# A two-block transformer in one kernel: the Fourier transforms' matrices loaded into X's place beside the projection

## What is computed

```python
def fourier_mix(u):
    B, S, _ = u.shape
    ug = u.reshape(B, S, F_GROUPS, F_GROUP_DIM).astype(jnp.float32)
    f = jnp.fft.fft2(ug, axes=(1, 3), norm="ortho").real
    return f.reshape(B, S, F_WIDTH).astype(u.dtype)

for l in range(DEPTH):
    last = l == DEPTH - 1
    h_x = modulate(x, sh1, sc1)
    h_c = modulate(xc, csh1, csc1)
    p_x = h_x @ lw["w_in"]
    p_c = h_c @ (lw["w_in"][:, :KV_COLS] if last else lw["w_in"])
    kv_c = kv_parts(p_c, lw, None)
    kv_x = kv_parts(p_x, lw, rope)
    ...
    mix_x = mixer(p_x, kv_all, lw, rope)   # y_f = fourier_mix(f_in) @ w_fo, and two attentions
    x = layer_norm(alpha * x + g1 * mix_x, ln1_g[l], ln1_b[l])
    ...
```

## Time and profile before

| | us |
|---|---|
| median of 3 runs | 3669.7 |
| lowest, highest | 3660.38, 3669.87 |
| profiled execution, time | 3670.66 |
| profiled execution, span | 3668.9 |

### The profile page before, as it was taken

The page is one execution under the profiler, slowest core; times in us unless marked ns, Lnnn a source line. Parts: engine busy times, 40 slices in busy tenths (PEclk is TensorE's granted clock), DMA queues, the critical chain, the costliest instruction groups (busy, mean ns, idle before and its releaser), DMA issues. The chain is left out here.

```text
span 3668.9 us, 37531 instructions
## 1 busy us (share of the span) xinstructions
PE 3231.2 (88%) x15004; PEld 2485.7 (68%) x15004; DVE 1937.6 (53%) x2904; ACT 1008.2 (27%) x1752; POOL 909.5 (25%) x596
## 2 busy tenths in 40 slices
PE   7988998999989999977898999599979778787698
PEld 4955666777478888775565664388869556576576
DVE  3654763444735555654474555467663546332354
ACT  3124761000221111221464001222231145411252
POOL 1003764221200000010377342200010326103353
PEclk9999999999999999989999999799989869788789
DMA  6411004443121111031102553222212200022100
GB/s 204 139 41 26 9 27 127 110 111 112 55 67 49 69 69 69 23 126 59 26 19 77 146 146 126 84 92 92 94 51 98 104 4 12 23 75 86 49 1 23
DMA packets 208413, 268.23 MB, mean 73 GB/s; under 512 B 29312, under 2 KB 136784, under 8 KB 207728
## 3 DMA queue, kind: packets, MB, share of 16 engines
q1 hardware_dynamic: 206160, 265.83, 22.7%
q10 hardware_dynamic: 2080, 0.01, 0.0%
HBM read 255.17 MB, written 10.52 MB: 72 GB/s over the span
## 5 line engine op out<-in xcount | busy, mean ns | idle before, releaser
L731 POOL TENSOR_TENSOR ht_lo<-HT,ht_hi 128x1024 fp32r<-128x1024 f32 x28 | 68.5, 2447 | 1144.5 <-ACT ht_hi L713 751.0
L1807 PE MATMUL ps<-ht_hi,w_hi 128*128 128x512 f32 (+1 forms) x768 | 275.4, 359 | 47.0 <-DVE w_lo L1925 32.9
L1807 PE MATMUL ps<-ht_lo,w_hi 128*128 128x512 f32 (+1 forms) x768 | 274.3, 357 | 0.0
L1807 PE MATMUL ps<-ht_hi,w_lo 128*128 128x512 f32 (+1 forms) x768 | 274.0, 357 | 0.0
L1817 PE MATMUL ps<-w_hi,a_hi 128*128 128x512 f32 x640 | 251.5, 393 | 4.3 <-DVE a_lo L1921 4.3
L1817 PE MATMUL ps<-w_lo,a_hi 128*128 128x512 f32 x640 | 250.5, 391 | 0.0
L1817 PE MATMUL ps<-w_hi,a_lo 128*128 128x512 f32 x640 | 250.3, 391 | 0.0
L363 PE MATMUL ps<-w_lo,ht_hi 128*128 128x320 f32 (+2 forms) x800 | 243.8, 305 | 0.0
L363 PE MATMUL ps<-gate_ht_hi,gate_w_hi 128*128 128x512 f32 (+1 forms) x576 | 228.4, 397 | 16.7 <-POOL w_lo L386 16.7
L1432 POOL TENSOR_TENSOR p_lo<-ring,p_hi 128x512 fp32r<-128x512 f32 x156 | 200.0, 1292 | 117.1 <-DVE p_hi L1387 88.6
L363 PE MATMUL ps<-U,ring 128*128 128x512 f32 (+1 forms) x576 | 217.9, 521 | 0.0
(11 more groups left out here) (394 smaller groups left out, 7964.1 us busy)
## 6 DMA issues: line engine op xcount, KB each, us to landing
ring<-w_dram SPq DMA_DIRECT2D x30, 2048.0 KB, 8.2
U<-w_ada_dram SPq DMA_DIRECT2D x80, 512.0 KB, 3.7
ring<-w_in_dram SPq DMA_DIRECT2D x48, 512.0 KB, 6.6
ring<-w_in_dram SPq DMA_DIRECT2D x8, 1280.0 KB, 5.9
ring<-a_w_in_dram SPq DMA_DIRECT2D x8, 1280.0 KB, 6.6
ring<-w_ada_dram SPq DMA_DIRECT2D x4, 2048.0 KB, 10.8
hi_scratch<-ht_hi SPq DMA_DIRECT2D x2, 3072.0 KB, 10.7
gate_ht_hi<-hi_scratch SPq DMA_DIRECT2D x8, 768.0 KB, 4.4
```

The lines of the kernel that those rows point to most:

```text
L731: pool.tensor_tensor(HT_LO[:, :, tokens], HT[:, :, tokens], HT_HI[:, :, tokens].bitcast(F32), ALU.subtract).then_inc(ht_ready.sem, 1)
L1807: last = pe.matmul(ps[:, g % 4, 0:c1 - c0], lhsT, rhs, start=(k + j == 0), stop=(k == KD - 1 and j == 2))
```

## The change

`DFT` becomes a view of `X` (its first four tiles). The two loads move from `fourier` into a new function, `fourier_loads`, called between the two projections; they wait for the normalised rows (`xn_ready`) and for the store of x, and raise a semaphore of their own, `dft_loaded`. The second projection loses its closing barrier. In its place TensorE waits for `dft_loaded` and for all evictions before the transforms, and VectorE waits for all evictions before the first half of its work.

```diff
--- before.py
+++ after.py
@@ -163,7 +163,7 @@
         MIX = view(0, KD, T)
         at_ot = NT * GATE_COL
         OT = view(at_ot, KD, T)
-        DFT = view(at_ot, 2 * XT, S)
+        DFT = X[:, 0:XT, :].rearrange("p t (a n) -> p (t a) n", n=S)
         at_ft = at_ot + KD * T
         FT = view(at_ft, 4, T)
         CTT = view(at_ft + 4 * T, 4, T)
@@ -203,6 +203,7 @@
         hi_ready = signal("hi_ready")
         ht_ready = signal("ht_ready")
         hi_stored = signal("hi_stored")
+        dft_loaded = signal("dft_loaded")
         hi_back = signal("hi_back")
         scales_ready = signal("scales_ready")
         wo_loaded = signal("wo_loaded")
@@ -812,6 +813,15 @@
         AB = view(at_ft + 4 * T, 2, S)
         TRIG = view(at_ft + 4 * T + 2 * S, 2, P)
 
+        def fourier_loads(now):
+
+            sp = nc.sync
+            sp.wait_ge(xn_ready.sem, now.xn + NT)
+            sp.wait_ge(x_stored.sem, x_stored.n)
+            sp.dma_start(DFT, A["dft_tokens"].rearrange("(t p) n -> p t n", p=P)).then_inc(dft_loaded.sem, 16)
+            sp.dma_start(TRIG[:, :, :], A["dft_features"].rearrange("(t p) n -> p t n", p=P)).then_inc(dft_loaded.sem, 16)
+            dft_loaded.n += 32
+
         def fourier(nt):
 
             parts = [(0, XT, S, 1)] + ([(XT, CT, M, S // M)] if nt > XT else [])
@@ -819,14 +829,11 @@
                 @b.sync
                 def _(sp):
                     sp.wait_ge(hi_stored.sem, hi_stored.n)
-                    sp.wait_ge(x_stored.sem, x_stored.n)
-                    sp.dma_start(DFT[:, :, :], A["dft_tokens"].rearrange("(t p) n -> p t n", p=P)).then_inc(loaded.sem, 16)
-                    sp.dma_start(TRIG[:, :, :], A["dft_features"].rearrange("(t p) n -> p t n", p=P)).then_inc(loaded.sem, 16)
-                    sp.wait_ge(loaded.sem, loaded.n + 32)
 
                 @b.tensor
                 def _(pe):
-                    pe.wait_ge(loaded.sem, loaded.n + 32)
+                    pe.wait_ge(dft_loaded.sem, dft_loaded.n)
+                    pe.wait_ge(evac_done.sem, evac_done.n)
                     g = 0
                     for t0, n, toks, step in parts:
                         for f in range(4):
@@ -869,7 +876,6 @@
                                            ACT.Copy).then_inc(evac_done.sem, 1)
             act_done.n += 1
             dve_done.n += 1
-            loaded.n += 32
             mm_done.n += 12 * len(parts)
             evac_done.n += 12 * len(parts)
 
@@ -925,6 +931,7 @@
                     (qg, RS[:, 24:24 + 8 * nq].rearrange("p (a b) -> p a b", b=8), HD)]
             @b.vector
             def _(dve):
+                dve.wait_ge(evac_done.sem, evac_done.n)
                 dve_chain.link(dve, dve.memset(RS[:, 0:72], 1.0))
                 for src, dst, width in sums:
                     squares(dve, src, dst, width)
@@ -3103,7 +3110,8 @@
                 pe.wait_ge(ht_ready.sem, now.ht + g + 1)
             project(NT, KV_COLS // 2, 0, P1, False, ready)
             early = Macs([(1, part, half) for part in (0, 1) for half in range(2)], 2, 0) if l == 0 else None
-            project(nq, REST // 4, KV_COLS, P1, macs=early)
+            fourier_loads(now)
+            project(nq, REST // 4, KV_COLS, P1, False, macs=early)
             fourier(nq)
             latents(NT, nq)
             up(NT, nq)
```

## The result

The changed kernel took 3646.9 us, median of 6 runs (3642.6 to 3651.7), beside 3669.3 us for the kernel before (6 runs, 3660.4 to 3669.9): a ratio of 0.9943, interval 0.9930 to 0.9956. It is 22.4 us faster, where 18.2 us were forecast. The profiled execution took 3642.91 us around a span of 3641.0. Lines of kernel.py stand one higher than before up to the evictions, seven higher from the transforms on: L364, L595, L803 and L844 are the L363, L594, L802 and L837 of before; the moved loads are L821 and L822, the root is L867, VectorE's second half L649.

A forecast was written before the change was run, and what follows sets the result against it. TensorE, busy 88% of the span, was taken as the bound, with gains from its idle time or slow clock. 11.8 + 13.9 - 6.1 - 1.4 = 18.2 us gave 3652 us, range 3641 to 3661.

The forecast's parts named there:

- Start of the transforms, layer 0: Layer 0, projection to transforms: they start 9.6 us earlier and save 2.2 us by the clock, 11.8 us together.
- if the clock stays up: Layer 0, first sixteen matmul records of the transforms: 7.03 instead of 9.25 us, 2.2 us saved.
- rival 2: Detour costs more: delay 9.8 us, clock loss 2.9, layer 0's transforms start at half clock (2.2); 3660 us, chance 0.17.
- Layer 1: Layer 1's transforms start 11.0 us earlier and save 2.9 by the clock; VectorE stays last, 13.9 us gained.
- The detour: Layer 0: moved loads delay the conditioning's loads queued behind them, and so TensorE, by 6.1 us (bounds 5.7 and 9.8).
- Rival 1: Layer 0: conditioning's loads share the engines and arrive in time, loads hidden free; 25.7 us gained, 3645 us, chance 0.15.
- The half clock behind the wait: Layer 0, after TensorE's wait for the second chunk's split: clock at half, costing 1.4 us, between 0 and 2.9.
- The four terms of the stages: Layer 0 gain 11.8, layer 1 gain 13.9, less detour 6.1 and half clock 1.4: 18.2 us.
- nothing after the stage depends on absolute time: After the stage in both layers: a barrier closes it and the rest only shifts.
- Rivals 3 and 4: Rival 3: moved loads hold conditioning 30 us, 3676, chance 0.03. Rival 4: something else holds the transforms, 3678, chance 0.03.

The follow-up runs named there:

- c1: The changed kernel a third time, unedited, beside two other versions on one chip: 3645.3 us.
- after_again: The changed kernel run once more, unedited: 3647.3 us.
- e1: Changed kernel with the two moved loads one chunk, about 18 us, earlier in SyncE's queue: 3643.0 us.
- c2: Same kernel as e1, run beside the changed kernel on the same chip: 3642.8 us.
- e4: Changed kernel with the barrier behind the second projection kept, the loads early: 3649.4 us in one run.
- e5: Changed kernel with 1.05 MB more loaded in layer 0 between the two moved loads: 3656.0 us in one run.
- e6: Changed kernel with layer 0's first two loads of the conditioning's weights issued ahead of the moved ones: 3648.2 us in one run.
- e7: e1 plus, in layer 0, the conditioning's last sixteen one-column products ahead of the projection's last tile: 3642.4 us.
- e8: e7 plus ScalarE's root for VectorE one copy earlier: 3641.3 us.
- c3: Same kernel as e8 (loads, small products and root all earlier), beside the changed kernel on the same chip: 3637.0 us.
- e9: Changed kernel, loads left in place, with only the sixteen small products ahead of the projection's last tile: 3651.1 us in one run.
- e2_layer1_only: The change in layer 1 alone; layer 0 keeps its barrier with the loads behind the projection, as before the change: 3651.3 us.

## Why the prediction was right, and where it was not

**Start of the transforms, layer 0: right.** Forecast: 2.3 us after the last product; it was 2.24. The full 11.8 us came in the first trace: the copies of the two kernels come closer by 11.82 us there. But the step "if the clock stays up" carried 2.2 of them, and it was given to rival 2 as a lesser possibility. Of the eight traces in which the sixteen small products stand right ahead of transforms that follow without a wait for a load (changed, c1, after_again, e1, c2, e4, e5, e6), the clock fell in six and the first sixteen records took 8.83 us. In the four with these products moved away (e7, e8, c3, e9) it stayed up each time. By chance a split this uneven would come in about 3 of 100 cases (an estimate that takes the traces as independent). The pause alone is not the reason: it was the shorter one where the clock fell. Nor are the small products alone: inside the projection, with full products right behind them, the same sixteen stand 46 times in the 14 traces, and the granted clock never fell there. What fell together with the clock is the two in a row, 2.1 us without a full product. The half clock is thus the commoner case over these eight traces, and costs 8.83 - 7.13 = 1.7 us; there this term is 9.25 - 8.83 = 0.4 us, not 2.2, and the stage gain of the changed kernel is the 16.1 us of after_again, not 18.3. The full clock came in two of its three own traces; that it came in the first was luck. Rival 2 had this mechanism right.

**Layer 1: right.** 13.9 us forecast, 13.8 measured, the same to a few hundredths in every trace with the edit; VectorE still ends the stage and waits 6.25 us for the root, so its first half was done by then, as forecast (in layer 0 too, with 3.14 us to spare), and moving the root alone (e8_root_earlier against e7_sums_earlier) brought 2.7 us there and 0.1 in layer 0.

**The detour: right in size and in cause.** Forecast 6.1 us more of waiting; it was 6.57, between the bounds of 5.7 and 9.8. VectorE's first product came at 118.82, as forecast (118.5). e5_one_mb_more gives the slope (2.9 us per 1.05 MB), e1_early and e6_conditioning_first the order of the queue: the loads' place decides who waits. By the Trainium skill, "DMA: Bandwidth & Descriptors", "Queues, rings and completion order", descriptors on an engine are consumed in ring order, and these traces agree. Rival 1, free hiding, would have needed the conditioning's loads to share the engines; its 3645 us lie within the scatter of the medians, but its mechanism did not occur, since its wait of 0.75 us was 7.32.

**The half clock behind the wait: mechanism right, size too large.** 1.4 us were taken as the middle of 0 and 2.9; it was 0.75. The clock did fall to 0.50, but VectorE's split, not TensorE, set the pace there. Its pace could have been read before: in the window from 126 to 130 us TensorE is busy for only 3.27 of 4 us.

**The sum.** The four terms of the stages give 11.8 + 13.8 - 6.6 - 0.7 = 18.3 us for 18.2 forecast. That they meet to 0.1 us is partly luck: the delay was 0.5 us too small and the half clock 0.7 us too large, and the warm start is in it. The measured medians differ by 22.4, 20.3 and 22.1 us in three groups of runs of the same kernel. The forecast said that nothing after the stage depends on absolute time and the rest only shifts; this step failed. The traces differ there in steps with different granted clocks, and so do traces of one kernel. In the profiled pair this part is 9.6 us, more than half of the 18.3. A difference of that size needs no change of the code: all kernels with the edit share the code outside the stages, and there their traces take between 3457.2 us (changed) and 3467.2 (e2_layer1_only), beside 3466.8 for before. In the table, median gain minus stage gain is +4.1, +4.2 and +3.8 us for the changed kernel, 0.0 and +0.1 for the earlier loads, -2.0, -3.7 and +2.0 for the kernels with the small products moved, -0.9 for layer 1 alone. Part of it is the one trace of before, which may be off by 2 us as the measure of L0. Whether the 4 us of the changed kernel are luck of such phases or a consequence of where its stages end in time stays open. Against the second speaks that the single runs of e5 and e9, with the loads in the same place, give -1.3 and -1.2, for it e4's +4.1; single runs can't settle it.

**Rivals 3 and 4.** The delay of 6.6 us is far from the 24 us from which the change would lose. The wait that the profile before put down to "issue" in layer 0 went with the load, so it was the load's: nothing else held the transforms.

## What to carry to other kernels

A load that is moved into the shadow of other work is paid for by whoever stands behind it in the same queue: look there for the next engine that already waits for a load, and price its delay as bytes ahead over the rate of the full engines (here 5.7 us by that, 6.6 measured). Then look for an earlier place in which nobody waits behind it; here that was one chunk, 18 us, earlier and gave back 6.3 us of the stage (2.6 and 4.3 us in the medians of two groups of runs). And once a wait is gone, read what TensorE does in the last microseconds before the stage: one-column products with a short wait behind them went with the loss of the full clock in six of eight traces here.

## What the runs showed of the hardware

- Sixteen one-column products (1.84 us) and a pause of 0.25 us ahead of full ones let the granted clock fall to 0.50 in six of eight traces, and a pause of 0.73 us with full products up to it in none of four; a barrier's pause of 1.44 us with full products ahead of it left it up in the one trace of e4_barrier_kept in layer 1. Inside the projection, with full products right behind them, the same sixteen products left the clock up in all 46 cases. So it takes both together here; that the emptiness of the products is the reason is suggested, not shown, as no run put a pause of 2.1 us in their place.
- A stretch at half clock cost 0.75 us where VectorE set the pace (layer 0's second chunk) and 1.7 us where TensorE did (the start of its transforms).
- The 2048 KB load landed 8.4 and 9.0 us after its issue with the engines free, 10.9 us beside others.
- Runs of one kernel on one chip lay up to 20 us apart (3638.9 to 3659.1), while the stages in question repeated to a few hundredths in layer 1 and to a microsecond or two in layer 0: a change of a few microseconds is measured better in its stage than in the whole time.
